# A final MoE combine and RMSNorm: four of nine tiles summed on TensorE, the 64-row tile first, the overflow count read sooner

## What is computed

```python
def _hier_moe(x, g, w_group, w_expert, w_gate, w_up, w_down):
    hf = _rmsnorm(x, g).reshape(bsz * s, D_MODEL)
    ...                                   # top-1 group of 4, then top-2 of 8 experts in it
    combine = jnp.sum(jax.nn.one_hot(expert_id, N_EXPERTS, dtype=f32) * gate_w[..., None], axis=1)
    act = jax.nn.silu(jnp.einsum("td,edf->tef", hf, w_gate)) * jnp.einsum("td,edf->tef", hf, w_up)
    out = jnp.einsum("tef,efd->td", act * combine[..., None].astype(act.dtype), w_down)

def _layer(...):
    ...
    x = x + _hier_moe(x, ...)

y_prompt = _rmsnorm(xp, g_final)          # y = x * rsqrt(mean(x * x) + 1e-6) * g
y_sample = _rmsnorm(xs, g_final)
```

## Time and profile before

| | us |
|---|---|
| median of three runs | 1249.03 (1247.46 to 1250.23) |
| profiled execution, time | 1249.47 |
| its span in the trace | 1247.6 |
| TensorE busy | 1122.6 (90% of the span) |
| VectorE busy | 494.6 (40%) |
| ScalarE busy | 250.4 (20%) |
| GpSimd busy | 82.3 (7%) |
| DMA, mean rate over the span | 168 GB/s |

### The profile page before, as it was taken

How to read it: one execution, slowest core, us unless ns; L and a number is a source line. 1 busy time by engine, 2 the same in 40 slices (tenths; PEclk the granted TensorE clock), 3 DMA queues, 4 the chain that set the end, 5 groups by cost and what they waited for, 6 DMA issues and landing times. The chain is left out here.

```text
span 1247.6 us, 14666 instructions
## 1 busy us (share of the span) xinstructions
PE 1122.6 (90%) x6081; PEld 619.8 (50%) x6081; DVE 494.6 (40%) x1011; ACT 250.4 (20%) x518; POOL 82.3 (7%) x104
## 2 busy tenths in 40 slices
PE   5999999999899999999999999997399999999930
PEld 4566766767654445666666545555333333333300
DVE  3585599746732223000266512224622122121138
ACT  5200311366611001010133210111001111111113
POOL 4000000001000000000000000000011111111000
PEclk9999999999999999999999999997589999999975
DMA  8009250493623002100214490004169999999657
GB/s 285 26 1 209 21 38 34 141 276 125 228 105 138 1 1 92 43 1 1 101 70 167 155 367 34 34 34 154 49 219 397 416 414 418 413 406 402 223 204 266
DMA packets 65365, 209.23 MB, mean 168 GB/s; under 512 B 13561, under 2 KB 22417, under 8 KB 57073
## 3 DMA queue, kind: packets, MB, share of 16 engines
q1 hardware_dynamic: 54528, 177.68, 40.2%
q0 software_dynamic: 10640, 30.55, 6.9%
q10 hardware_dynamic: 128, 0.03, 0.0%
HBM read 187.05 MB, written 28.53 MB: 173 GB/s over the span
## 5 line engine op out<-in xcount | busy, mean ns | idle before, releaser
L751 PE MATMUL bank<-arena 128*128 128x512 f32 x480 | 208.8, 593 | 0.7 <-DVE arena L1538 0.7
L584 PE MATMUL bank<-arena 128*128 128x360 f32 (+1 forms) x576 | 180.0, 474 | 2.5 <-DMA arena<-in_w_in 1.5
L955 PE MATMUL bank<-arena 128*32 128x512 f32 x1536 | 170.7, 596 | 0.0
L584 PEld LDWEIGHTS bank<-arena 128*128 128x128 f32 x576 | 110.3, 193 | 68.8 <-issue 4.0
L751 PEld LDWEIGHTS bank<-arena 128*128 128x128 f32 x480 | 90.1, 190 | 109.1 <-issue 108.1
L769 PE MATMUL bank<-arena 128*128 128x360 f32 (+1 forms) x384 | 117.4, 468 | 0.0
L1036 ACT ACTIVATE arena<-bank 128x360 f32<-128x360 f32 (+7 forms) x117 | 51.0, 437 | 304.8 <-PE bank L584 130.9
L955 PEld LDWEIGHTS bank<-arena 128*32 128x32 f32 x1536 | 47.5, 110 | 105.6 <-issue 105.2
L769 PEld LDWEIGHTS bank<-arena 128*128 128x128 f32 x384 | 72.8, 190 | 43.7
L1563 DVE TENSOR_TENSOR arena<-arena,bank 128x512 f32<-128x512 f32 (+1 forms) x36 | 24.8, 688 | 171.5 <-PE bank L751 148.7
L971 PE MATMUL bank<-arena 128*32 128x512 f32 x768 | 86.9, 592 | 5.6 <-DMA arena<-in_w_down 5.0
(11 more groups left out here) (362 smaller groups left out, 1205.6 us busy)
## 6 DMA issues: line engine op xcount, KB each, us to landing
arena<-in_w_gate SPq DMA_DIRECT2D x32, 1024.0 KB
arena<-in_w_up SPq DMA_DIRECT2D x32, 1024.0 KB
arena<-in_w_down SPq DMA_DIRECT2D x32, 1024.0 KB
arena<-in_ck SPq DMA_DIRECT2D x8, 1024.0 KB, 6.1
arena<-in_cv SPq DMA_DIRECT2D x8, 1024.0 KB, 5.3
arena<-work_moe SPq DMA_DIRECT2D x16, 512.0 KB, 10.4
arena<-in_w_in SPq DMA_DIRECT2D x3, 2048.0 KB, 14.9
arena<-in_x SPq DMA_DIRECT2D x8, 512.0 KB, 7.0
```

What stands on the lines that cost most here:

```text
L584: last = nc.tensor.matmul(b[:, 0:w], win[slot][:, k, m * P:m * P + P], ht[:, k, c0:c0 + w], start=k == 0, stop=k == KD - 1)
L751: last = nc.tensor.matmul(b[0:ROWS[i], :], lhs(k, i), w[0][:, k, nh * 512:nh * 512 + 512], start=k == 0, stop=k == KD - 1)
L955: last = nc.tensor.matmul(bank[2 + j % 2][t0:t0 + QT, :].rearrange("p (h n) -> p h n", h=2), xgt[j % 2][:, k, t0:t0 + QT], gu[e % GUB][:, ...
```

## The change

Three things are changed, all at the end of the program.

1. GpSimd tests the overflow count right after its last store is issued. The waits for `y_st0` and `y_st1` move into the branch that is skipped, and to SyncE, ahead of the final stage's loads.
2. Loads, sums and stores take the order FORDER = 8, 0, 1, ... 7. Tile 8 is the one with 64 rows.
3. Tiles 1, 3, 5 and 7 (FPE) are summed on TensorE. VectorE builds eight diagonal matrices `fdg` (the identity times a column of `wcomb`, 128x128). TensorE adds into two PSUM banks per tile identity x `xres`, then diagonal x `fy` for both expert choices. ScalarE squares the two banks apart, brings the second sum of squares into the bias of the root, and VectorE makes the product from the banks in two halves. The other five tiles go as before.

The semaphores of tiles 6, 7 and 8 are ones that served `xres` earlier, and so start at 32.

```diff
@@ sync
             sp.wait_ge(sem["fin_x"], 1)
-            for i in range(NT):
+            for b in range(2):
+                sp.wait_ge(sem[f"y_st{b}"], 16 * NR // 2)
+            for i in FORDER:
                 r = ROWS[i]
                 for c in range(2):
-                    sp.dma_start(fy[i][0:r, c, :], W["moe"][c * TOK + i * P:c * TOK + i * P + r, :]).then_inc(sem[f"f_in{i}"], 16)
-            for o in range(NT):
-                sp.wait_ge(sem["f_out"], o + 1)
+                    sp.dma_start(fy[i][0:r, c, :], W["moe"][c * TOK + i * P:c * TOK + i * P + r, :]).then_inc(sem[FIN[i][0]], 16)
+            for n, o in enumerate(FORDER):
+                sp.wait_ge(sem["f_out"], n + 1)
@@ gpsimd
-            for b in range(2):
-                pool.wait_ge(sem[f"y_st{b}"], 16 * NR // 2)
             pool.wait_ge(sem["ctl_ok"], 1)
             with pool.If(pool.value_load(ctl[0:1, XT:XT + 1], min_val=0, max_val=XT) > 0):
+                for b in range(2):
+                    pool.wait_ge(sem[f"y_st{b}"], 16 * NR // 2)
@@ tensor
+            pe.wait_ge(sem["ya_ok"], NR)
+            pe.wait_ge(sem["yd_done"], NR)
+            pe.wait_ge(sem["fin_x"], 1)
+            for j, i in enumerate(FPE):
+                for hf in range(2):
+                    nc.tensor.matmul(bank[2 * j + hf][:, :], ident[:, :], xres[:, i, hf * 512:hf * 512 + 512], start=True, stop=False)
+            pe.wait_ge(sem["f_dg"], 2 * len(FPE))
+            for j, i in enumerate(FPE):
+                pe.wait_ge(sem[FIN[i][0]], FIN[i][1])
+                for hf in range(2):
+                    for c in range(2):
+                        last = nc.tensor.matmul(bank[2 * j + hf][:, :], fdg[:, j, c, :], fy[i][:, c, hf * 512:hf * 512 + 512], start=False, stop=c == 1)
+                last.then_inc(sem["f_pe"], 1)
@@ scalar
+                if i in FPE:
+                    j = FPE.index(i)
+                    act.wait_ge(sem["f_pe"], j + 1)
+                    link(nc.scalar.activation(squaresf[:, 0:512], bank[2 * j][:, :], ACT.Square, accum_out=ssq[:, i:i + 1]))
+                    link(nc.scalar.activation(squaresf[:, 512:1024], bank[2 * j + 1][:, :], ACT.Square, accum_out=srs[:, j:j + 1]))
+                    link(nc.scalar.activation(srs[:, j:j + 1], srs[:, j:j + 1], ACT.Identity, scale=1.0 / D, bias=zero1[:, 1:2]))
+                    nc.scalar.activation(rstd[:, i:i + 1], ssq[:, i:i + 1], ACT.Sqrt, scale=1.0 / D, bias=srs[:, j:j + 1]).then_inc(sem["f_std"], 1)
@@ vector
+                if i in FPE:
+                    j = FPE.index(i)
+                    for hf in range(2):
+                        cols = slice(hf * 512, hf * 512 + 512)
+                        last = V.scalar_tensor_tensor(xres[:, i, cols], bank[2 * j + hf][:, :], rstd[:, i:i + 1], gfin[:, cols], MUL, MUL)
+                    last.then_inc(sem["f_out"], 1)
...
+            for j, i in enumerate(FPE):
+                for c in range(2):
+                    V.tensor_scalar(fdg[:, j, c, :], ident[:, :], wcomb[:, i, c:c + 1], None, MUL).then_inc(sem["f_dg"], 1)
             dve.wait_ge(sem["gf_in"], 16)
-            for i in range(NT):
+            for i in (8, 0):
                 fsum(i)
-                if i >= 1:
-                    fout(i - 1)
-            fout(NT - 1)
+            for i in (8, 0):
+                fout(i)
+            for i in (2, 4, 6):
+                fsum(i)
+                fout(i - 1)
+                fout(i)
+            fout(7)
```

More of the change, by code:

```diff
@@ L55 @@
 ht_full htm_ok d_full ya_ok yd_done y_st0 y_st1 x_go xw_in xg_in xt_full xt_free xgu_full xsilu_ok xprod_ok
-xht_full xhtm_ok xd_full xya_ok xyd_ok xy_st f_in0 f_in1 f_in2 f_in3 f_in4 f_in5 f_in6 f_in7 f_in8 gf_in f_sum f_std f_out f_st
+xht_full xhtm_ok xd_full xya_ok xyd_ok xy_st f_in0 f_in1 f_in2 f_in3 f_in4 f_in5 gf_in f_dg f_pe f_sum f_std f_out f_st
 fin_x"""
@@ L236, in hybrid_layer @@
         fy = [reg(2048 * s, 2, D) for s in range(NT)]
+        FORDER, FPE = (8, 0, 1, 2, 3, 4, 5, 6, 7), (1, 3, 5, 7)
+        fdg = reg(R_R, len(FPE), 2, P)
+        FIN = [(f"f_in{i}", 32) if i < 6 else (f"x_res{i - 6}", 48) for i in range(NT)]
         gfin, squaresf = reg(18432, D), reg(19456, D)
@@ L1240, in _ @@
                     y_first(0, "xya_ok")
-            for i in range(NT):
+            sums = 0
+            for i in FORDER:
                 r = ROWS[i]
-                act.wait_ge(sem["f_sum"], i + 1)
-                link(nc.scalar.activation(squaresf[0:r, :], xres[0:r, i, :], ACT.Square, accum_out=ssq[0:r, i:i + 1]))
-                nc.scalar.activation(rstd[0:r, i:i + 1], ssq[0:r, i:i + 1], ACT.Sqrt, scale=1.0 / D, bias=zero1[0:r, 1:2]).then_inc(sem["f_std"], 1)
+                if i in FPE:
[5 more added lines that the diff above has]
+                    nc.scalar.activation(rstd[:, i:i + 1], ssq[:, i:i + 1], ACT.Sqrt, scale=1.0 / D, bias=srs[:, j:j + 1]).then_inc(sem["f_std"], 1)
+                else:
+                    sums += 1
+                    act.wait_ge(sem["f_sum"], sums)
+                    link(nc.scalar.activation(squaresf[0:r, :], xres[0:r, i, :], ACT.Square, accum_out=ssq[0:r, i:i + 1]))
+                    nc.scalar.activation(rstd[0:r, i:i + 1], ssq[0:r, i:i + 1], ACT.Sqrt, scale=1.0 / D, bias=zero1[0:r, 1:2]).then_inc(sem["f_std"], 1)
         @block.vector
@@ L1804, in fsum @@
                 r = ROWS[i]
-                dve.wait_ge(sem[f"f_in{i}"], 32)
+                dve.wait_ge(sem[FIN[i][0]], FIN[i][1])
                 link(V.scalar_tensor_tensor(xres[0:r, i, :], fy[i][0:r, 0, :], wcomb[0:r, i, 0:1], xres[0:r, i, :], MUL, ADD))
@@ L1810, in fout @@
                 r = ROWS[i]
-                dve.wait_ge(sem["f_std"], i + 1)
+                dve.wait_ge(sem["f_std"], FORDER.index(i) + 1)
                 link(V.reciprocal(rstd[0:r, i:i + 1], rstd[0:r, i:i + 1]))
-                V.scalar_tensor_tensor(xres[0:r, i, :], xres[0:r, i, :], rstd[0:r, i:i + 1], gfin[0:r, :], MUL, MUL).then_inc(sem["f_out"], 1)
+                if i in FPE:
[4 more added lines that the diff above has]
+                    last.then_inc(sem["f_out"], 1)
+                else:
+                    V.scalar_tensor_tensor(xres[0:r, i, :], xres[0:r, i, :], rstd[0:r, i:i + 1], gfin[0:r, :], MUL, MUL).then_inc(sem["f_out"], 1)
+            for j, i in enumerate(FPE):
+                for c in range(2):
+                    V.tensor_scalar(fdg[:, j, c, :], ident[:, :], wcomb[:, i, c:c + 1], None, MUL).then_inc(sem["f_dg"], 1)
             dve.wait_ge(sem["gf_in"], 16)
-            for i in range(NT):
+            for i in (8, 0):
                 fsum(i)
-                if i >= 1:
-                    fout(i - 1)
-            fout(NT - 1)
+            for i in (8, 0):
[5 more added lines that the diff above has]
+            fout(7)
 _INS = {"x": (TOK, D), "mem": (NM, D), "wk": (D, D), "wv": (D, D), "w_in": (D, 3 * DH), "w_glu": (DH, DH)}
```

## The result

The gain is the one that was forecast. The median is 1241.72 us (1239.68 to 1242.88, six runs) against 1250.83 (1247.46 to 1253.0, six runs) for the kernel before on the same chips: 9.1 us less, ratio 0.9927, 95% interval 0.9909 to 0.9944. A second comparison later gave 0.9925 (0.9909 to 0.9941). The forecast was 1240.1, 8.9 us less, range 1237.6 to 1242.9.

A forecast was written before the change was run, and what follows sets the result against it. VectorE's chain bounds the final stage, the DMA queue behind it. With the change the queue ends it: 1200.6 plus 31.9, 1.0 and four stores at 1.2 gives 1238.3, plus 0.4 span 1238.7; median 1240.1, range 1237.6 to 1242.9.

The forecast's parts named there:

- What bounds the kernel: In the final stage, VectorE's chain fills 35.9 us before the change, with the DMA queue as the wall behind it.
- this sign: Final stage: if the store of the last VectorE product lands in 2.6 us, the queue was no bound.
- Early read: GpSimd's overflow test runs under the last expert store's flight; loads start at 1200.6, 1.5 us gained, bounds 0 and 1.6.
- 64-row tile first: Start of the final stage: tile 8 lands at 1206.8, VectorE starts 1.5 us sooner, and the end gets cheaper.
- TensorE: Final stage, tiles 1, 3, 5, 7: matmuls of 0.87 us, 3.5 us per tile; net 9.6 us off VectorE.
- my slower rival: Final stage slower than before, TensorE as bound, decided from a matmul of 1.8 us; at 2.0 us median 1252; chance 0.04.
- VectorE's chain: Final stage: first sum at 1206.9, tile 7's product at 1234.6 against 1244.3; span 1237.6 if VectorE sets the end.
- The queue: Final stage's DMA: all loads and four stores in 31.9 us, remaining stores until 1238.3; span 1238.7; chance 0.47.
- The gain: Whole kernel: span 1247.6 falls to 1238.7, 8.9 us less; median 1240.1.
- VectorE's chain alone: Rival for the final stage: VectorE's chain, not the queue, is the end; span 1237.6, median 1239.0; chance 0.2.
- tile 7 wasn't late: Rival for the final stage's loads: stores delay tile 7's second half again; span 1240.5, median 1241.9; chance 0.14.

The follow-up runs named there:

- one cut alone: Changed kernel with the first of VectorE's two sums left out in tiles 8, 0, 2, 4, 6, or with half the loads: medians 1240.83 and 1238.38 us.
- both together: Changed kernel without that first sum in tiles 8, 0, 2, 4, 6 and with half the loads: median 1233.92 us, ratio 0.9871.
- The first profile: The changed kernel, profiled first: final stage, from last expert store's issue to end of span, 39.4 us.
- the second profile: The changed kernel, unchanged, profiled again: final stage 41.1 us, median 1240.51 us, ratio 0.9925.
- one sum less: Changed kernel without the first of VectorE's two sums in tiles 8, 0, 2, 4, 6: final stage 40.0 us, median 1240.83 us.

## Why the prediction was right, step by step

- **What bounds the kernel: right, and closer than forecast.** Before the change VectorE's chain is the end. With it, VectorE and the DMA queue lie about 1 us apart: in the medians one cut alone gains 0 to 3 us on the change, both together 6.6 to 7.4. The forecast gave the queue the end by 1.1 us. The first profile has it so (tile 7's load, then 0.3 us in the last store); in the second TensorE's clock held VectorE up, and the queue was no bound. I had named this sign: a last store that lands in 2.6 us.
- **Early read: right.** 3.29 us from the last store's issue to the first load against 3.4 forecast and 4.88 before, 1.6 us gained for 1.5. The test was over sooner than I said: GpSimd's copy ended 1.3 us after the store's issue, not 2.6. Both are under the store's flight.
- **64-row tile first: right in kind, its end mis-sized.** Half the rate for half the rows holds. The first sum came 5.1 us after the first load, forecast 6.3: I took the 3.7 us that tile 0's loads took besides their wire time for a constant, and it was smaller in most later runs.
- **TensorE: the price was right by two mistakes.** I divided 208.8 us by 480 records of L751 and called a record a matmul. The trace has two records for one of these matmuls: 4 of tile 1 show as x8, 8 with the identity as x16. So a matmul costs 0.87 us at 2.4 GHz and 1.74 at 1.2, not 0.435 and 0.87. And the clock wasn't at 1.2 GHz, as I had said for the whole stage: it rose in 1206 to 1207 while the identity matmuls ran. Twice the price at twice the clock gives the 3.5 us that I wrote and the 3.67 and 3.70 measured. That is luck. Where the clock fell, in the second profile, tile 1's four matmuls took 5.38 us and held VectorE up. Without the rise, a matmul of 1.74 us would have stood just under the 1.8 from which my slower rival decides. I gave that rival 4 in 100, on the ground that 1.8 was more than twice either bound. That ground was false, and the chance too small.
- **VectorE's chain: right in the first profile,** 27.7 us forecast and measured, with a product from PSUM of 0.16 + 1.41 us (1.5 forecast) and a wait for tile 7's root (0.9 forecast, 1.14 measured). The second took 29.6, by the clock.
- **The queue: too long by 2.0 us.** From the first load to the last landing I forecast 1238.3 - 1200.6 = 37.7 us; it took 1237.8 + 2.9 - 1205.0 = 35.7. I took 31.9 us for all loads and four stores from the kernel before. In it the last load, issued at 1213.0, landed after 17.2 us:

```profile
L408 SPq DMA_DIRECT2D arena<-work_moe x1: 1082/1082/1082, 1213.0 to 1213.0; - x1
...
DMA to landing us min/median/max: 17.2/17.2/17.2
```

That is 28.1 us after the first issue; with the change it was 1230.3 - 1205.0 = 25.3, and the stores behind it took 0.8 more than forecast. With the tiles in the order 0 to 8 the last load landed 26.1 to 28.1 us after the first issue (five profiles), with the 64-row tile first 25.3 to 26.2 (six profiles). So the order makes the same loads shorter, by 1.3 us in the mean, which my sum for the queue put at nothing; the rest of the 2.0 is variation from profile to profile, and its cause stays open.

- **The gain: right in part by luck.** The stage was forecast at 41.5, 8.9 less; 39.4 and 41.1 were measured. The forecast's queue was too long by 2.0 us, and it had no loss from a falling clock; in the medians these two errors work against each other, and how much of each is in them isn't known. The kernel before was 1.8 us slower beside the change than in the runs shown ahead, so the total is 1.6 over the forecast though the gain is off by 0.2 only.
- **Rivals.** The gain isn't VectorE's chain alone, and tile 7 wasn't late with the change; it is late when the 64-row loads stand behind it, as the change without the order shows.

## What to carry to other kernels

When one engine's chain is shortened, measure the next wall from the same windows, and take its length from a stretch that has the same neighbours: here the queue's 31.9 us held a delay, some 1.3 us in the mean, that the new order removed. Count a group's records against the instructions in the program before dividing a busy time by them. Offload to an idle TensorE can rest on its clock: look at the granted clock in the window of each burst, in more than one profile, since the same kernel may have both levels. And profile a kernel twice before a difference in one stage is given to an experiment's edit: two profiles of one kernel differed by 1.7 us here, as much as several of the edits.

## What was not expected of the hardware

- A float32 matmul of 512 columns shows as two records and costs 0.87 us at 2.4 GHz (3.70 us for four) and twice that at 1.2 GHz.
- In the final stage the clock held over a gap of 3.13 us in TensorE's work, and fell in another run of the same kernel behind a gap of 4.06 us. With one sum less it fell behind 3.55 us, with TensorE alone behind 3.27 and in the change without the order behind 2.72 us. So the length of the gap alone doesn't decide it.
- A 64-row load halves the rate of the whole queue at a full busy share (191 and 238 GB/s against 410), and a 128-row load in flight beside it came 1.3 us late or more.
- The same first loads of the stage had tile 0 ready after 5.05 to 6.29 us. Its cause stays open.
